# GpSimd in TensorE's place: root rows of three norms and the normaliser of the odd mixer

## The reference, cut to what matters

```
def rmsnorm(x, g):
    return x * rsqrt(mean(x * x, -1) + EPS) * g
...
for l in range(2):
    y = even_mixer(rmsnorm(x, g[0]), ...) if l == 0 else odd_mixer(rmsnorm(x, g[0]), ...)
    x = x + rmsnorm(y, g[1])
    x = x + rmsnorm(square(relu(rmsnorm(x, g[2]) @ w1)) @ w2, g[3])
...
# odd mixer, by head: scores weighted by exp of the gates
num = scores @ v
den = sum(scores, -1)
out = num / maximum(abs(den), exp(-m_row))
```

## Time and profile before

| what | value |
|---|---|
| median of 3 runs | 968.39 us (967.96 to 969.23) |
| the profiled execution | 968.83 us |
| its span, first to last instruction | 967.0 us |
| granted TensorE clock, mean | 0.997 of full speed |
| PE busy | 959.6 us, 99% of the span |
| DVE busy | 696.0 us, 72% |
| ACT busy | 541.1 us, 56% |
| POOL busy | 35.4 us, 4% |
| DMA | 187.27 MB, 194 GB/s |

### The profile page before, as it was taken

How to read it: one execution, slowest core, us unless ns; L and a number is a source line. 1 busy time by engine, 2 the same in 40 slices (tenths; PEclk the granted TensorE clock), 3 DMA queues, 4 the chain that set the end, 5 groups by cost and what they waited for, 6 DMA issues and landing times.

```text
span 967.0 us, 13003 instructions
## 1 busy us (share of the span) xinstructions
PE 959.6 (99%) x5144; PEld 828.3 (86%) x5144; DVE 696.0 (72%) x941; ACT 541.1 (56%) x733; POOL 35.4 (4%) x24
## 2 busy tenths in 40 slices
PE   9999999999999999999999999999999999999997
PEld 8898888888888889988888888887888888888886
DVE  5989646688778867866688778878555888755474
ACT  7844464664554546645675455459446566545433
POOL 0000000000000000000000000000000000002000
PEclk9999999999999999999999999999999999999999
DMA  9953525367776774434467877774855444466611
GB/s 328 307 175 131 174 88 196 131 219 250 256 251 221 244 244 140 165 131 131 152 218 232 268 234 245 260 211 130 269 175 194 154 151 154 175 218 222 212 45 44
DMA packets 122864, 187.27 MB, mean 194 GB/s; under 512 B 5331, under 2 KB 88756, under 8 KB 122804
## 3 DMA queue, kind: packets, MB, share of 16 engines
q1 hardware_dynamic: 122368, 186.05, 58.1%
q10 hardware_dynamic: 436, 0.40, 0.1%
HBM read 185.37 MB, written 1.06 MB: 193 GB/s over the span
## 4 chain that ended last, share of the span: by engine, by line
PE 99%; ACT 0%; issue 0%; DVE 0%; ACTq 0%
PE bank L677 97%; PE bank L933 1%; PE bank L1023 0%; PE bank L1106 0%; PE bank L876 0%; PE bank L942 0%; PE bank L740 0%; ACT arena L1845 0%; ACT sd L1845 0%; DVE arena L1227 0%; DVE x L1227 0%; ACT hx L1845 0%; PE bank L1048 0%; PE bank L961 0%; DVE rs L1835 0%
## 5 line engine op out<-in xcount | busy, mean ns | idle before, releaser
L1227 DVE TENSOR_TENSOR wl<-raw,wh 128x2048 fp32r<-128x2048 f32 (+1 forms) x157 | 357.0, 2275 | 134.7 <-ACT wh L1850 105.1
L1850 ACT CAST wh<-raw 128x2048 fp32r<-128x2048 f32 x155 | 294.9, 1912 | 129.2 <-PE bank L677 127.0
L677 PE MATMUL bank<-hx,wh 128*128 128x512 f32 (+1 forms) x1280 | 295.3, 363 | 0.1
L677 PEld LDWEIGHTS bank<-hx,wh 128*128 128x128 f32 x1280 | 220.2, 190 | 31.2 <-issue 0.7
L677 PE MATMUL bank<-wh,hx 128*128 128x512 f32 x576 | 185.7, 396 | 0.6 <-ACT hx L1845 0.5
L677 PE MATMUL bank<-hx,wl 128*128 128x256 f32 x1088 | 174.3, 282 | 0.0
L677 PEld LDWEIGHTS bank<-hx,wl 128*128 128x128 f32 x1088 | 156.7, 190 | 8.8
L677 PE MATMUL bank<-wh,yh 128*128 128x512 f32 (+1 forms) x420 | 163.4, 389 | 0.0
L677 PE MATMUL bank<-wl,yh 128*128 128x512 f32 (+1 forms) x420 | 162.8, 388 | 0.0
L677 PE MATMUL bank<-wh,yl 128*128 128x512 f32 (+1 forms) x420 | 162.6, 387 | 0.0
L677 PEld LDWEIGHTS bank<-wh,hx 128*128 128x128 f32 x576 | 108.6, 189 | 24.5 <-issue 1.6
(11 more groups left out here) (190 smaller groups left out, 709.0 us busy)
## 6 DMA issues: line engine op xcount, KB each, us to landing
raw<-in_mlp_w SPq DMA_DIRECT2D x64, 1024.0 KB, 5.2
raw<-in_w_in SPq DMA_DIRECT2D x40, 1024.0 KB, 5.1
raw<-in_ev_w_in SPq DMA_DIRECT2D x19, 1024.0 KB, 5.4
raw<-in_w_ada SPq DMA_DIRECT2D x12, 1024.0 KB, 5.0
raw<-in_od_w_in SPq DMA_DIRECT2D x12, 1024.0 KB, 5.1
raw<-in_ev_w_out SPq DMA_DIRECT2D x6, 1024.0 KB, 4.8
raw<-in_od_w_out SPq DMA_DIRECT2D x4, 1024.0 KB, 4.8
raw<-in_w_o_conv SPq DMA_DIRECT2D x4, 1024.0 KB, 4.8
```

The lines of the kernel that those rows point to most:

```text
L677: return eng.matmul(o, l, r, start=start, stop=stop, skip_group_check=True)
L1227: return eng.tensor_tensor(o, x, y, op)
L1850: eng.copy(part(wh, u), part(raw, u)).then_inc(S["hi"], 1)
```

## The change

The six spreading products (two for each of norms 1 to 3) and DVE's three copies of their bank go. POOL has `root_row(n)` in their place: for each half t it multiplies the identity by the broadcast root column (128 by 128), so that each partition holds its own token's root in its own column, and adds 256 columns over all partitions with `partition_all_reduce`, straight into `x_row[n]`. DVE waits for `x_row` where it copied before. `f_up`'s wait before bank 3 becomes one for low parts of x of the norm, which were ready long before.

The twelve products with ones go too. POOL has `den_sums(g)` for each pair of heads g: it copies the columns of t < 128, adds the two source halves of t >= 128, adds 512 columns over all partitions, and multiplies by the identity, so that each partition keeps only its own token. DVE then has two reductions over the free dimension in place of the copy of 8 columns, and waits for POOL as well as for PE.

```
@@ tensor @@
-                if n in LATE:
-                    x_spread(n)
...
                     elif first == 2:
-                        eng.wait_ge(S["x_row"], 2 * layer + 1)
+                        eng.wait_ge(S["hl"], h_count(2 * layer + 1, 0, KT - 1))
...
                 for h in range(HEADS):
-                    s = m_s[:, h, :]
-                    mm(PS[4][:, 64 + h:65 + h], s[:, 0:P], ones[:, :], True, True)
-                    mm(PS[4][:, 68 + h:69 + h], s[:, P:2 * P], ones[:, :], True, False)
-                    mm(PS[4][:, 68 + h:69 + h], s[:, SEQ:SEQ + P], ones[:, :], False, True)
...
@@ vector @@
                     eng.wait_ge(S["mout"], HEADS)
-                    link(tensor(gden[:, :, :], PS[4][:, 64:72].rearrange("p (t h) -> p t h", t=2)))
+                    eng.wait_ge(S["den_own"], 2)
+                    eng.tensor_reduce(gden[:, :, 0:2].rearrange("p t h -> p h t"), den_own(0), AX_X, ALU.add)
+                    link(eng.tensor_reduce(gden[:, :, 2:4].rearrange("p t h -> p h t"), den_own(1), AX_X, ALU.add))
...
                 if SECOND.get(u) in LATE:
-                    eng.wait_ge(S["x_bc"], SECOND[u])
-                    tensor(x_row[SECOND[u]], PS[3][:, 0:SEQ]).then_inc(S["x_row"], 1)
                     eng.wait_ge(S["x_row"], SECOND[u])
@@ gpsimd @@
+            def root_row(n):
+                for t in range(TT):
+                    eng.wait_ge(S["x_rs"], 2 * (n - 1) + t + 1)
+                    eng.tensor_tensor(row_part[:, tokens(t)], ident[:, :], rs[:, t:t + 1].broadcast_to([P, P]),
+                                      ALU.mult).then_inc(S["x_own"], 1)
+                eng.wait_ge(S["x_own"], 2 * n)
+                eng.partition_all_reduce(x_row[n], row_part, P, bass.bass_isa.ReduceOp.add).then_inc(S["x_row"], 1)
+            def den_sums(g):
+                s, part = m_s[:, 2 * g:2 * g + 2, :], den_part(g)
+                eng.wait_ge(S["ms"], 2 * g + 2)
+                eng.tensor_copy(part[:, :, 0:P], s[:, :, 0:P]).then_inc(S["den_fold"], 1)
+                eng.tensor_tensor(part[:, :, P:SEQ], s[:, :, P:SEQ], s[:, :, SEQ:SEQ + P], ALU.add).then_inc(S["den_fold"], 1)
+                eng.wait_ge(S["den_fold"], 2 * g + 2)
+                eng.partition_all_reduce(den_total(g), part.rearrange("p h t -> p (h t)"), P,
+                                         bass.bass_isa.ReduceOp.add).then_inc(S["den_sum"], 1)
+                eng.wait_ge(S["den_sum"], g + 1)
+                own = den_own(g).rearrange("p h t s -> p (h t) s")
+                eng.tensor_tensor(own, own, ident[:, :].unsqueeze(1).broadcast_to([P, 4, P]), ALU.mult).then_inc(S["den_own"], 1)
...
+                if GROUP_AT.get(u) in LATE:
+                    root_row(GROUP_AT[u])
+                if u == at("mog"):
+                    den_sums(0)
+                    den_sums(1)
```

More of the change, by code:

```diff
@@ L337, in build @@
             "up_half up_low up_sum x_row x_hsq x_hb d_x0 d_x1 d_rows d_small d_tables d_causal d_wg d_u d_bias d_out d_grow d_gate piece fin_c "
-            "const d_masks masks cols colsT step_dve lo_ada mod x_ssq x_sd x_rs x_bc x_w x_n x_t ada_sum hh hl hpart wk hturn "
+            "const d_masks masks cols colsT step_dve lo_ada mod x_ssq x_sd x_rs den_fold den_sum den_own x_own x_w x_n x_t ada_sum hh hl hpart wk hturn "
             "ysq yb ysd yh yl_pool yl_dve yl6 acc mturn "
@@ L455, in build @@
         x_row = {1: view(10240, SEQ), 2: tables[:, 384:384 + SEQ], 3: view(10240, SEQ)}
+        row_part = view(10496, SEQ)
         def x_rms(n):
@@ L471, in ml_bank, with den_part, den_total, den_own @@
             return PS[(5, 6, 2, 3)[2 * (h // 2) + t]][:, (h % 2) * RET_DV:(h % 2 + 1) * RET_DV]
+        def den_part(g):
+            return wf[:, 512 + 1024 * g:1024 + 1024 * g].rearrange("p (h t) -> p h t", h=2)
+        def den_total(g):
+            return wf[:, 1024 - 512 * g:1536 - 512 * g]
+        def den_own(g):
+            return den_total(g).rearrange("p (h t s) -> p h t s", h=2, t=TT)
         def m_bank(t, half):
@@ L913, in b_piece @@
                 return m
[L915 to L922, removed]
             def x_turn(n, t):
@@ L1078, in ml_out @@
                 for h in range(HEADS):
-                    s = m_s[:, h, :]
-                    mm(PS[4][:, 64 + h:65 + h], s[:, 0:P], ones[:, :], True, True)
-                    mm(PS[4][:, 68 + h:69 + h], s[:, P:2 * P], ones[:, :], True, False)
-                    mm(PS[4][:, 68 + h:69 + h], s[:, SEQ:SEQ + P], ones[:, :], False, True)
                     for t in range(TT):
-                        m = values_out(ml_bank(t, h), t, m_v, h, s)
+                        m = values_out(ml_bank(t, h), t, m_v, h, m_s[:, h, :])
                     m.then_inc(S["mout"], 1)
```

## The result

| | before | after |
|---|---|---|
| median | 968.34 us (967.96 to 969.23, 4 runs) | 1003.8 us (1003.4 to 1004.25, 4 runs) |
| profiled execution / its span | 968.83 / 967.0 us | 1003.72 / 1001.9 us |
| granted TensorE clock, mean | 0.997 | 0.981 |

The changed kernel takes 1.0365 times as long (95% interval 1.0352 to 1.0378): 35.5 us more on the medians, 34.9 on the spans. The forecast was 27.6 more, with a range that ended at 1003. The result lies 0.8 us outside.

A forecast was written before the change was run, and what follows sets the result against it. PE was taken as the bound, busy 959.6 of 967.0 us. Spared products -3.4, stall +29.3 and clock +1.7 gave +27.6 us on 968.83, so 996 us, range 965 to 1003.

The forecast's parts named there:

- nearly free: Rival for POOL's switches: they cost almost nothing, L under 0.7 us, time 965.4 to 967.0 us; chance 0.20.
- both directions are paid: Counter to the rival that only switches to the reduction cost: two count in the chain, 979.6 us; chance 0.13.
- ACT's 1.28 us: Rival: a POOL switch is a nearby reload like ACT's table load, 7.7 us of stall, 974.8 us; chance 0.07.
- The roots' rows: POOL's rows for norms 1 to 3: lateness costed at nothing, at most 0.5 us twice.
- L: Price of one POOL switch, taken as 5.6 us from a 1 KB transfer amid the weights; ends 0.01 and 8 us.
- end of the first copy: POOL's 256-column copy starting the normaliser's chain: held until DVE's low part ends at 423.17, then 0.5 us, ending 423.7.
- rest of the chain on POOL: Normaliser's additions, reductions, products and second copy on POOL after the first copy, without switches: 11.6 us.
- X: Time POOL is done with the normaliser and DVE can go on: 435.3 + 5 L.
- from X to PE going on: DVE's reductions and small operations 2.4 us, then ACT's root, table load and bank 0 evacuation 2.3 us: 4.7 us.
- stall: PE's wait before unit `mog` 2, X + 4.7 - 438.7 = 5 L + 1.3 us, 29.3 us with L = 5.6.
- clock after the stall: PE restarts at its lower clock level, full clock after 3.4 us: 1.7 us lost, ends 0 and 3.4.
- the full 3.4 us: PE time spared by removed products: norms' spreads 0.36 us three times, heads' products with ones 0.58 us four times.

The follow-up runs named there:

- roots_only: Changed kernel with the normaliser's twelve products with ones and DVE's copy of `den` put back, roots' rows still on POOL: 967.91 us, ratio 0.9992 to before.
- early_load: Changed kernel with one instruction calling for the TENSOR_TENSOR library on POOL ahead of the first wait for `m_s`: 996.15 us, one run.
- the probe: Kernel before, plus a train of 128-column reductions and products on scratch tiles on idle POOL after unit `mv`, which nobody waits for: 971.28 us, one run.
- den_only: Changed kernel with the roots' spreading products on PE and DVE's copies put back, normaliser's sums still on POOL: 1003.82 us, one run.
- grouped: `early_load` with both head pairs' steps done one kind at a time, leaving two switches in the chain: 984.55 us, one run.
- one_kind: Changed kernel with all POOL's new TENSOR_TENSOR operations made copies, so values differ from the reference: 964.9 us, ratio 0.996 to before.
- split_both: Changed kernel with DVE adding source halves and multiplying by the identity, for normaliser and roots; POOL keeps reductions and copies: 964.58 us, ratio 0.9961 to before.
- select: Changed kernel with masks made by AFFINE_SELECT on POOL and source halves added by DVE's last reductions: 967.99 us, ratio 0.9991 to before.

## Why the prediction was wrong

**What held.** The bound, the place and the mechanism: PE has no slack, the switches that the builder adds fall in a chain that PE waits for, all five are paid, and the kernel becomes slower (by 2.8% in the forecast, by 3.65% as measured). The rivals fell: switches are not nearly free, both directions are paid, and none took as little as ACT's 1.28 us. The roots' rows were costed at nothing, and `roots_only` shows no loss from them.

**The step that failed** is the price of a switch, L = 5.6 us, "from the nearest rows". It was the time of a 1 KB transfer from issue to landing, and the five gaps took 5.69 to 8.94 us, 35.3 in all where 5 L was 28.0: +7.3 us. Even L for a fetch in two steps, 8 us, lay below the longest. The row shows how long a small transfer takes to land; it says nothing of a switch. No row of before could have told its price, since both switches stood in idle time. Here the range had to carry the doubt, and mine gave 0.10 to what lies above 1003, although one L is counted five times, so that a miss of 1.5 us in it is one of 7 in the time. A range up to the forecast's own upper end, L = 8 and 1008 us, would have held the result.

The GPSIMD Engine Reference of the Trainium skill, section 2.1 (Instruction dispatch), gives 5.95 us for the first call after a load. The two gaps ahead of reductions in the chain, 5.80 and 5.69 us, agree with it to 0.3 us; those ahead of TENSOR_TENSOR, 7.14 to 8.94, don't. By its figure the sum, as an estimate, would have been 1.8 us above mine and still 5.5 short. And where it puts the price on the first call, `early_load` shows that the work is done at the switching instruction.

**The other terms** of the chain, each with what it measured:

| term | forecast | measured |
|---|---|---|
| end of the first copy, us | 423.7 | 422.98 |
| five switches | 28.0 | 35.3 |
| rest of the chain on POOL | 11.6 | 10.8 |
| POOL ready, X | 463.3 | 469.04 |
| from X to PE going on | 4.7 | 4.9 |
| start of PE's stall | 438.70 | 437.38 |
| stall | 29.3 | 36.56 |
| clock after the stall | 1.7 | 2.0 |

The reduction of 512 columns took 3.25 us and not 3.58: with 1.79 for 256, and 2.26 us for two of 128 in the probe, there is a small fixed part, by estimate some 0.3 us. The copy was held by DVE's low part as the subtraction of the earlier trace rows was, and took 2.39 us. Stall: 36.56 - 29.3 = 7.3 us, of which X gave 5.7, the way from X to PE 0.2, and PE's standing 1.3 us earlier than forecast the rest.

**The sum, term by term.** From the forecast's 27.6 to the 34.9 us of the spans: +7.3 for the switches, -0.8 for the rest of the chain on POOL, -0.3 for the first copy, which ended 0.26 us behind DVE's low part and not 0.5, +0.2 for the way to PE, +0.3 for the clock, +0.3 for norm 3's spreads, whose 0.4 us brought 0.1 (PE is 35.04 behind at the transposes and 34.9 at the end), and +0.3 for those of norms 1 and 2, whose 0.7 us brought 0.45 at the head of the chain (the low part ended at 422.72 and not at 423.17).

The last term needs a word. These spreads lie ahead of the chain, and the sum took them off in full while it read the chain's start and the stall's start from the trace of before. Time spared ahead of a wait is lost where the end of the wait is set elsewhere. Here POOL's chain starts from scores that PE makes, so it moves with PE, and so does the end of the wait. `den_only`, which has the spreads back, shows it: its first copy starts 0.72 us later than the 420.59 of after.

```profile
421.31 2.39 POOL L2271 COPY work<-arena 128x256 f32<-128x256 f32 x1 [97.41 <-DVE arena L1240]
```

So taking the full 3.4 us off was sound. That all terms but the switches come to nothing together is luck.

**Where PE's earlier 1.3 us came from.** The forecast had PE 2.3 us ahead where the stall begins, for the products with ones alone; at the start of `mog` 1 it was 3.9 ahead. The products with ones spared 2.7 us (from 427.80 to 435.47 before, 7.67 us; 4.99 with the twelve products with the values alone). The spreads gave 0.4. And the stretch at the lower clock behind the gates did not occur in this execution, which gave 1.6, of which 0.8 was lost again right behind it. That stretch comes and goes: between 415.5 and 419 us the granted clock was 0.52 in the trace of before, 0.60 in those of `roots_only` and `grouped`, and 1.00 in the other nine. So no part of the change accounts for it, and where PE stands when the wait begins changes the stall and not the time: the end of the wait is POOL's.

## What to carry to other kernels

On GpSimd the order of the kinds of operation counts more than the operations: look in the built queue for the switching instructions, and price each at 5.5 to 9.6 us, as measured here, unless POOL is idle there. Keep a chain within one kind (copies and selections stood beside a reduction without a switch), hand two-operand steps to the vector engine, group what is left by kind, and issue the load before the wait. A price that the trace of before hides in idle time can be measured by a train of small operations that nobody waits for, and until then it belongs in the range as many times as the chain pays it.

## What the runs showed of the hardware that was not expected

- **The cost of a switch has no row of its own.** The switching instructions last 1 to 98 ns in the trace; the cost shows only as idle time put down to "issue" ahead of the next operation, 5.5 to 9.6 us. The transfers of instructions that the page lists don't grow with it either: 41 packets on queue 8 in every one of these kernels, and 19 to 21 on queue 14. How the code comes, if it is a transfer, is not shown.
- **VectorE and GpSimd hold each other up, in both directions.** POOL's copy of 256 columns took 0.39 us alone and 2.39 beside a low part on DVE. The reverse, from DVE's timeline in `one_kind`, where the low part takes 4.23 us instead of 2.28 while POOL's reduction from 423.20 to 426.43 runs:

```profile
420.23 2.28 DVE L1222 TENSOR_TENSOR wl<-raw,wh 128x2048 fp32r<-128x2048 f32 x1
...
423.36 4.23 DVE L1222 TENSOR_TENSOR wl<-raw,wh 128x2048 fp32r<-128x2048 f32 x1
```

  The GPSIMD Engine Reference of the Trainium skill, section 8 (Key points), says that the two share their SBUF interfaces and that DVE's instructions with two SBUF inputs contend. The low parts are such, and the trace agrees. In the probe, five operations of DVE between 376 and 418 us took 0.2 to 0.7 us longer each than in the kernel before, 1.8 together; DVE began its last steps for the gates 1.65 us later (418.45 for 416.80), and PE waited 2.0 for DVE. `split_both`'s first reduction, beside a low part and an addition on DVE, took 5.15 us in place of 3.25.
- **Selections run under either library.** In `select` the first AFFINE_SELECT comes ahead of the load for the reductions (norm 1 has one gap of 5.77 us, between the two), and later ones come after reductions without a gap (427.07 and 433.31 in its timeline above).
- **Unsettled:** why a load for TENSOR_TENSOR costs more than one for the reduction, and how much of a load's price the weight stream sets.
